# Forgetting attention with split one-pass score products and one shared step for the last queries

## The reference, cut to what matters

```
q = rmsnorm(q, q_gain) * (Dh ** -0.5);  k = rmsnorm(k, k_gain)
c = cumsum(log_sigmoid(f + b_f))              # one row of 272 values per head
s = q @ k.T + c[query] - c[key];  s = where(key <= query, s, -inf)
o = softmax(s) @ v
o = o * sigmoid(gate);  out = o @ w_out
```

## Time and profile before

| | us |
|---|---|
| median of 3 runs | 5328.38 |
| lowest, highest | 5323.99, 5332.9 |
| the profiled execution: time | 5331.09 |
| the profiled execution: span | 5329.3 |
| first attention stage (first POOL instruction to the end of the last gate product) | 3318.25 to 3464.27 |
| second attention stage | 4927.7 to 5073.64 |

### The profile page before, as it was taken

How to read it: one execution, slowest core, us unless ns; L and a number is a source line. 1 busy time by engine, 2 the same in 40 slices (tenths; PEclk the granted TensorE clock), 3 DMA queues, 4 the chain that set the end, 5 groups by cost and what they waited for, 6 DMA issues and landing times. The chain is left out here.

```text
span 5329.3 us, 57668 instructions
## 1 busy us (share of the span) xinstructions
PE 4142.0 (78%) x19870; PEld 2896.1 (54%) x19870; DVE 3009.1 (56%) x6151; ACT 1916.2 (36%) x4273; POOL 1076.5 (20%) x982
## 2 busy tenths in 40 slices
PE   7874677777777777746777768988789967888989
PEld 3663463232232323735323237488789866888489
DVE  7447546676666664475676643354554733544354
ACT  7433323333333333333333334243343421434243
POOL 0015114444444441041444420000100011000000
PEclk9986789999999999868999989599889977999589
DMA  9310139999999996305999963044235400453044
GB/s 365 133 60 0 44 140 420 419 417 416 415 407 417 412 419 241 99 17 188 420 420 415 416 265 109 1 153 152 84 117 164 139 1 1 149 156 116 1 139 139
DMA packets 205764, 1143.63 MB, mean 215 GB/s; under 512 B 24016, under 2 KB 25616, under 8 KB 106784
## 3 DMA queue, kind: packets, MB, share of 16 engines
q0 software_dynamic: 110592, 805.36, 36.7%
q1 hardware_dynamic: 94880, 334.58, 19.0%
HBM read 1138.73 MB, written 1.05 MB: 214 GB/s over the span
## 5 line engine op out<-in xcount | busy, mean ns | idle before, releaser
L1065 PE MATMUL bank<-rows,diag 128*128 128x512 f32 x2304 | 1091.1, 619 | 395.6 <-ACT diag L1120 388.3
L348 PE MATMUL bank<-x_high,w_high 128*128 128x272 f32 (+2 forms) x3560 | 1107.4, 311 | 100.8 <-DVE x_low L414 100.5
L348 PE MATMUL bank<-x_low,w_high 128*128 128x272 f32 (+2 forms) x3560 | 1096.3, 308 | 0.0
L348 PE MATMUL bank<-x_high,w_low 128*128 128x272 f32 (+2 forms) x3560 | 1095.4, 308 | 0.0
L400 DVE TENSOR_TENSOR w_low<-ring,w_high 128x1024 fp32r<-128x1024 f32 (+2 forms) x541 | 645.6, 1200 | 707.9 <-ACT w_high L375 707.9
L1065 PEld LDWEIGHTS bank<-rows,diag 128*128 128x128 f32 x2304 | 426.7, 194 | 1053.0 <-ACT diag L1120 598.8
L1237 DVE CUSTOM_DVE_ANT_0 junk<-rows,hT 128x1024 f32<-128x1024 f32 x576 | 705.7, 1225 | 412.1 <-DMA rows<-in_peer_uv,expert 396.1
L1028 POOL DMA_INDIRECT rows<-in_peer_uv,expert x576 | 622.2, 1080 | 1160.0 <-PE bank L1065 807.3
L348 PEld LDWEIGHTS bank<-x_high,w_high 128*128 128x128 f32 x3560 | 684.0, 192 | 151.0 <-issue 58.2
L375 ACT CAST w_high<-ring 128x1024 fp32r<-128x1024 f32 (+2 forms) x541 | 552.3, 1027 | 583.0 <-PE bank L348 555.1
L348 PEld LDWEIGHTS bank<-x_low,w_high 128*128 128x128 f32 x3560 | 686.3, 193 | 20.5
(11 more groups left out here) (346 smaller groups left out, 4965.7 us busy)
## 6 DMA issues: line engine op xcount, KB each, us to landing
ring<-in_w_gate_up SPq DMA_DIRECT2D x176, 512.0 KB, 3.4
ring<-in_w_mod SPq DMA_DIRECT2D x96, 512.0 KB, 5.7
ring<-in_w_in SPq DMA_DIRECT2D x64, 512.0 KB, 3.4
ring<-in_fox_w_in SPq DMA_DIRECT2D x64, 512.0 KB, 3.4
ring<-in_w_down SPq DMA_DIRECT2D x64, 512.0 KB, 3.5
ring<-in_peer_wq SPq DMA_DIRECT2D x32, 512.0 KB, 3.4
ring<-in_gdn_w_in SPq DMA_DIRECT2D x32, 512.0 KB, 3.8
ring<-in_w_down SPq DMA_DIRECT2D x32, 384.0 KB, 3.8
```

The source lines that it names most:

```text
L348: last = pe.matmul(k.bank[c % BANKS][:, 0:nt], w[:, slot, cols], xx[:, t, t0:t0 + nt], start=(t == 0 and n_pass == 0), stop=(t == KT - 1 a ...
L1065: last = pe.matmul(k.bank[2 * (i % 2) + half][:, :], diag[:, n % 4, :], slot(n)[:, D + half * 512:D + (half + 1) * 512], start=(e == 0), s ...
```

## The change

Three things, in both attention stages. First, q and k are split into float32r halves (`q_high`, `q_low`, `k_high`, `k_low`) by a cast on ACT and a subtraction on DVE per chunk, and a score product becomes three float32r products on 64 rows; the decay is one more float32r product of a broadcast column of ones for the head (`pick`) with `c_rows`, which holds the high parts and the rests of the running sums. The query's own term c[query] is left out. The scores are made negated (the gain of q has a minus sign), so the row's minimum serves directly as the bias of an exponential with scale -1, and the negation step is gone. Second, a step "head" does both blocks of 128 queries of a head in one PSUM bank: 128 keys for the first, 256 for the second. Third, the last 16 queries of four heads share one step "last": their queries are placed in four strips of 32 stationary columns, zero outside the head's rows (`end_high`, `end_low`), and six products of 272 columns on 128 rows over two chunks, with one for the decay, give the scores of the four heads together. So 48 steps become 20. POOL first fills the four zeroed tiles, which all other engines wait for; the DMA and `picked` are gone. The constants grow by 272 columns.

```diff
-    put("causal", np.concatenate([np.zeros((P, 2 * P)), np.where(i[None, :] > i[:, None], NEG, 0.0)], 1))
+    put("causal", np.concatenate([np.zeros((P, 2 * P)), np.where(i[None, :] > i[:, None], -NEG, 0.0)], 1))
+    put("causal_last", np.where(np.arange(T2)[None, :] > 2 * P + (i % 32)[:, None], -NEG, 0.0))
+    put("pick2", sum((i[:, None] == np.arange(FOX_HEADS)[None, :] + r) for r in (0, 32, 64, 96)))
...
-                order(dve.tensor_scalar(k.qgain[:, 0:1], gq, DK_FOX ** -0.5, None, ALU.mult))
+                order(dve.tensor_scalar(k.qgain[:, 0:1], gq, -(DK_FOX ** -0.5), None, ALU.mult))
...
-                order(dve.tensor_scalar(f[:, 2, :], f[:, 1, :], -1.0, None, ALU.mult))
...
-    steps = [(h, i) for h in range(FOX_HEADS) for i in range(3)]
+    steps = []
+    for g in range(4):
+        steps += [("last", g)] + [("head", 4 * g + j) for j in range(4)]
...
+        q_high, q_low = (sbuf(k, es, n, [P, KD, 2 * P], F32R) for n in ("q_high", "q_low"))
+        end_high, end_low = (sbuf(k, es, n, [P, KD, P], F32R) for n in ("end_high", "end_low"))
+        k_high, k_low = (sbuf(k, es, n, [P, KD, T2], F32R) for n in ("k_high", "k_low"))
+        c_rows = sbuf(k, es, "c_rows", [P, T2], F32R)
+        pick = sbuf(k, es, "pick", [P, FOX_HEADS], F32R)
+        pick_last = sbuf(k, es, "pick_last", [P, 4 * P], F32R)
+        sc = sbuf(k, es, "sc", [P, 3, 384])
+        pr = sbuf(k, es, "pr", [P, 3, 384])
+        pT = sbuf(k, es, "pT", [P, 2, 384])
+        pL = sbuf(k, es, "pL", [P, 2, 384])
+        least = sbuf(k, es, "least", [P, 3, 2])
+        total = sbuf(k, es, "total", [P, 3, 2])
+        inv = sbuf(k, es, "inv", [P, 3, 2])
...
+        def end_of(j):
+            return slice((j % 2) * DK_FOX, (j % 2 + 1) * DK_FOX), slice(j // 2, KD, 2), slice(32 * j, 32 * j + META)
         @block.gpsimd
         def _(pool):
+            for ap in (end_high, end_low):
+                pool.tensor_copy(ap[:, :, :], k.causal[:, 0:P].unsqueeze(1).broadcast_to([P, KD, P])).then_inc(s.cleared, 1)
+            pool.tensor_copy(c_rows[:, :], k.causal[:, 0:1].broadcast_to([P, T2])).then_inc(s.cleared, 1)
+            pool.tensor_copy(pick_last[:, :], k.causal[:, 0:1].broadcast_to([P, 4 * P])).then_inc(s.cleared, 1)
...
+            kind, h = steps[n]
+            bank = k.bank[n % 3]
             if n >= 3:
+                pe.wait_ge(s.lowest, n - 2)
+            if kind == "last":
+                pe.wait_ge(s.low, 4 * (h + 1))
+                if n == 0:
+                    pe.wait_ge(s.ends_low, 4)
+                for c in (2 * h, 2 * h + 1):
+                    for i, (qq, kx) in enumerate(((end_high, k_high), (end_high, k_low), (end_low, k_high))):
+                        pe.matmul(bank[:, 0:T2], qq[:, c, :], kx[:, c, :], start=(c == 2 * h and i == 0), stop=False)
+                if n == 0:
+                    pe.wait_ge(s.rows, 4)
+                pe.matmul(bank[:, 0:T2], pick_last[:, h * P:(h + 1) * P], c_rows[:, :], start=False, stop=True).then_inc(s.scored, 1)
+                return
+            own = slice((h % 2) * DK_FOX, (h % 2 + 1) * DK_FOX)
+            for t0, nk in ((0, P), (P, 2 * P)):
+                out = bank[:, t0:t0 + nk]
+                for i, (qq, kx) in enumerate(((q_high, k_high), (q_high, k_low), (q_low, k_high))):
+                    pe.matmul(out, qq[own, h // 2, t0:t0 + P], kx[own, h // 2, 0:nk], start=(i == 0), stop=False)
+                last = pe.matmul(out, pick[own, h:h + 1].broadcast_to([DK_FOX, P]), c_rows[own, 0:nk], start=False, stop=True)
+            last.then_inc(s.scored, 1)
...
+            cuts = (0, 128, 256) if kind == "head" else (0, 128, 256)
+            for j, k0 in enumerate(cuts):
+                nk = P if kind == "head" else TILES2[j][1]
+                last = pe.transpose(bank[0:nk, j * P:(j + 1) * P], pr[:, n % 3, k0:k0 + nk], k.ident)
             last.then_inc(s.turned, 1)
...
+            vv = lambda j: v[0:TILES2[j][1], j, h * DK_FOX:(h + 1) * DK_FOX]
+            t = pT[:, h % 2, :]
+            pe.matmul(bank[lo:lo + DK_FOX, 0:2 * P], vv(0), t[:, 0:2 * P], start=True, stop=False)
+            pe.matmul(bank[lo:lo + DK_FOX, P:2 * P], vv(1), t[:, 2 * P:3 * P], start=False, stop=True)
+            for j in range(3):
+                nk = TILES2[j][1]
+                at = j * P + 32 * (h % 4)
+                last = pe.matmul(bank[lo:lo + DK_FOX, 2 * P:T2], vv(j), pL[0:nk, (h // 4) % 2, at:at + META], start=(j == 0), stop=(j == 2))
             last.then_inc(s.mixed, 1)
...
+            def make_low(c):
+                for x, high, low in ((q, q_high, q_low), (kk, k_high, k_low)):
+                    dve.wait_ge(s.high, 2 * c + (1 if x is q else 2))
+                    n = low.shape[2]
+                    dve.tensor_tensor(low[:, c, :], x[:, c, 0:n], high[:, c, :].bitcast(F32), ALU.subtract).then_inc(s.low, 1)
+            dve.wait_ge(s.cleared, 4)
+            for j in range(4):
+                dve.wait_ge(s.ends_high, j + 1)
+                own, chunks, cols = end_of(j)
+                dve.tensor_tensor(end_low[own, chunks, cols], q[own, chunks, 2 * P:T2], end_high[own, chunks, cols].bitcast(F32),
+                                  ALU.subtract).then_inc(s.ends_low, 1)
+            make_low(0)
+            make_low(1)
+            dve.wait_ge(s.rows, 2)
+            for row in (32, 96):
+                dve.tensor_tensor(c_rows[row:row + FOX_HEADS, :], f[:, 1, :], c_rows[0:FOX_HEADS, :].bitcast(F32),
+                                  ALU.subtract).then_inc(s.rows, 1)
...
+                    for i, (cols, mask) in enumerate(parts(n)):
+                        if mask is None:
+                            allowed = k.const("causal_last")
+                        else:
+                            allowed = k.causal[:, mask:mask + cols.stop - cols.start]
+                        last = dve.tensor_tensor_reduce(sc[:, b, cols], k.bank[b][:, cols], allowed, 1.0, -NEG, ALU.add, ALU.min,
+                                                        least[:, b, i:i + 1])
+                    last.then_inc(s.lowest, 1)
+                if n < NS and n % 5 in (2, 3) and n // 5 < 3:
+                    make_low(2 * (n // 5) + n % 5)
...
+            def make_high(c):
+                act.copy(q_high[:, c, :], q[:, c, 0:2 * P]).then_inc(s.high, 1)
+                act.copy(k_high[:, c, :], kk[:, c, :]).then_inc(s.high, 1)
+            act.wait_ge(s.cleared, 4)
+            for j in range(4):
+                own, chunks, cols = end_of(j)
+                act.copy(end_high[own, chunks, cols], q[own, chunks, 2 * P:T2]).then_inc(s.ends_high, 1)
+            make_high(0)
+            make_high(1)
+            act.copy(pick_last[0:48, :].rearrange("p (h n) -> p h n", n=32), k.const("pick2")[0:48, :].unsqueeze(2).broadcast_to([48, FOX_HEADS, 32]))
+            act.copy(pick[:, :], k.const("pick2"))
+            for row in (0, 64):
+                act.copy(c_rows[row:row + FOX_HEADS, :], f[:, 1, :]).then_inc(s.rows, 1)
...
+                    for i, (cols, _) in enumerate(parts(n)):
+                        last = act.activation(pr[:, b, cols], sc[:, b, cols], ACT.Exp, scale=-1.0, bias=least[:, b, i:i + 1],
+                                              accum_out=total[:, b, i:i + 1])
+                    last.then_inc(s.exped, 1)
+                if n < NS and n % 5 in (1, 2) and n // 5 < 3:
+                    make_high(2 * (n // 5) + 1 + n % 5)
...
+                    if kind == "head":
+                        if h >= 2:
+                            act.wait_ge(s.mixed, h - 1)
+                        last = act.copy(pT[:, h % 2, :], bank[:, 0:384])
+                    else:
+                        if h >= 2:
+                            act.wait_ge(s.mixed, 4 * (h - 1))
+                        act.copy(pL[:, h % 2, 0:256], bank[:, 0:256])
+                        last = act.copy(pL[0:META, h % 2, 256:384], bank[0:META, 256:384])
```

More of the change, by code:

```diff
@@ L1376, in fox_attention @@
     H = k.H
-    steps = [(h, i) for h in range(FOX_HEADS) for i in range(3)]
+    steps = []
+    for g in range(4):
+        steps += [("last", g)] + [("head", 4 * g + j) for j in range(4)]
     NS = len(steps)
[L1379 to L1397, removed]
+    heads_to = [sum(kind == "head" for kind, _ in steps[:n + 1]) for n in range(NS)]
@@ new lines, in fox_attention, with parts @@
+    lasts_to = [sum(kind == "last" for kind, _ in steps[:n + 1]) for n in range(NS)]
+    with ExitStack() as es, stage(k, "attention", "cleared ends_high ends_low high low rows scored lowest exped rcp normed turned copied mixed gated") as (block, s):
+        q_high, q_low = (sbuf(k, es, n, [P, KD, 2 * P], F32R) for n in ("q_high", "q_low"))
[11 more added lines that the diff above has]
+        inv = sbuf(k, es, "inv", [P, 3, 2])
+        def parts(n):
+            if steps[n][0] == "head":
+                return [(slice(0, 128), 256), (slice(128, 384), 128)]
+            return [(slice(0, T2), None)]
+        def end_of(j):
```

(43 more changed lines are left out.)

60 lines of the change are left out of this document (8 added, 52 removed).

## The result

The kernel after takes 5172.74 us in the median of 4 runs (5161.70, 5165.12, 5180.35 and 5181.45), the kernel before 5328.49 (5323.99 to 5332.90) beside it: a ratio of 0.9707 with a 95% interval of 0.9682 to 0.9731.

The account below looks back on a forecast made before the run. PE's own product list at 1.2 GHz was taken to bound the attention stages: 5331.1 - 94.8 + 0.4 = 5236.7, less 2 x 15.6 and 2 x 1 for the clock: 5203.5, less 2.7: 5201, stated as 5204; 8-in-10 range 5160 to 5256.

Parts of the forecast that it names:

- The 128-column pass: Attention scores: a float32r pass of 128 columns costs 0.213 us at 1.2 GHz, set by its weight load.
- rival of a dear pass: Attention scores: 128-column passes cost 0.43 us each, 27.7 us in all; 5261 at the old clock; chance 0.14.
- that of four cycles a column: Attention scores: float32r passes on 64 rows cost like float32 products, making the kernel slower, +54 us, 5383; chance 0.03.
- A head and the shared step: PE's list in an attention stage at 1.2 GHz: 5.07 us a head, 2.72 a shared step, 92.0 in all.
- Begin of the stage: Attention setup: POOL fills, then casts and rests; PE's first product comes 5.8 us into the stage.
- The clock: Attention stages: granted clock rises from 0.50 at a shared step and mostly holds, 15.6 us less a stage; chance 0.45.
- rival of an unchanged clock: Attention stages: the clock stays at 0.50, 5234 us by the median; chance 0.27.
- That of a clock full nearly from the start: Attention stages: full clock nearly from the start, 59 us a stage, 5158 us in all; chance 0.10.
- I take 83 as the mean of both stages: Attention stages: mean length 83 us with a clock rise part of the way, 15.6 below 98.6.
- the three places foreseen: Clock rise at a shared step about 24, 47 or 70 us into an attention stage; stage near 67, 79 or 91.
- The constants' 272 columns, 0.14 MB, are 0.4 us more of loading: Loading of the constants: the wider tile adds 0.4 us, if nothing else hides it.
- term of the projections: Projections behind the attention stages: starting at clock 1.00 saves 1 us on average each, 2 x 1 in all.

Follow-up runs that it names:

- after_again: The changed kernel run once more, unaltered, beside two plain-heads orders on one chip: 5164.47 us over 5 runs, ratio 0.9702.
- plain_heads: Changed kernel with each head's three float32r score passes replaced by one plain float32 product, the split kept for the shared step: 5156.37 us, ratio 0.9673.
- before with the warm-up: Kernel before, with eight float32 products on 128 rows at the head of PE's attention-stage list: 5275.39 us over 4 runs, ratio 0.9888.

## Why the prediction was right, and where it was off

**What bounds it.** PE's own list bounds the stages before and after. Right. At 1.00 PE waits for DVE a little (1.0 us from 3335 to 3375).

**The 128-column pass.** 0.213 forecast, 0.21 measured, with a load on 64 rows as long as on 128. By the rule of the Trainium skill ("TensorE: Matmul & The Clock Gate", section "LDWEIGHTS (loading the stationary operand)") it would have been 0.107; at 0.50 the runs differ from it for these float32r loads. The rival of a dear pass falls, and that of four cycles a column too: 256 columns in 0.21 are one cycle a column.

**A head and the shared step.** 4.98 for 5.07 and 2.52 for 2.72: PE's list at 0.50 is 16 x 4.98 + 4 x 2.52 = 89.8 for 92.0. At 1.00 a head is 2.78 (3347.32 to 3350.10 from product to product) for 2.7. The kernel without the shared step tests the sum at 0.50: its heads are 4.97 apart (4904.22 to 4909.19), 16 of them and its begin of 8.5 make 88.0, where its stages take 87.0 and 87.2. So such sums are good to 1 or 2 us. Begin of the stage 6.0 for 5.8.

**The clock.** The mechanism held: 0.50 in the heads, a rise behind a shared step, kept in one stage of the profile and lost after 10 us in the other. That it is the shared step is shown by the kernel without one (0.50 in both its stages but for 1.0 us) and by the 12 rises counted there. What in it counts, the rows or the dense stream, isn't told apart. The rival of an unchanged clock falls. That of a clock full nearly from the start falls for this kernel, but its price of 59 us a stage is borne out by a relative: the one stage that ran at 1.00 from its setup on took 57.9, with plain heads, earlier casts and the warm-up. The Trainium skill (same page, section "Why this matters for your kernels") ties the full clock to an engine kept busy without pause; after, 52.00 of 52 us busy at 0.50 disagree with it, as the earlier trace rows did.

**The step that was mis-sized** is "I take 83 as the mean of both stages". The profiled execution has 77.6, the one of after_again 67.3. The rise came at the earliest of the three places foreseen, 23.2 to 24.4 us into the stage, in both stages of both profiles; I had weighed all three alike. What remains luck is the fall behind it. In us, forecast against profiled execution: 10.7 of 22.0 lie in the attention stages (136.7 saved, not 126.0). By the parts above some 4 of them are the list's (96.6 a stage at 0.50, where 98.6 stood) and some 7 the clock's (38 for 31.2), each to within 2 us or so.

The forecast's sums have slips beside that. A group of four heads and a shared step that takes 12 us for 23 saves 11, so from 98.6 the three places of the rise give 66, 77 and 88 us, not 67, 79 and 91; the profile's first stage took 66.1. The setup's parts add up to 5.7. The 5158 of the full clock is by the profiled execution; by the median it would be 5155, less another 2 with the projections. Half of the dear case is 5248, not 5256. The break-even of the slower rival is at 3.0 cycles a column, not 3.2. None of them changes which rival falls.

**The step that was wrong** is "The constants' 272 columns, 0.14 MB, are 0.4 us more of loading": 8.8 of the 22.0. The expert stages got 8.4 shorter, and the constants alone do 7 of it. No row of the profile before bore on it, since it compares one layout only. The last 2.5 us lie in the other stages. The term of the projections, 2 us saved, didn't come either: the last product of the projection starts 30.1 and 29.2 us behind the attention stage before, 30.4 and 30.6 after. In the first the clock fell at 3378.3, before the projection's products began, in the second it was at 0.50 up to 4931.3. So 6.2 us were saved elsewhere, which wasn't followed.

**From execution to median** the forecast took 2.7 off and put 3.2 on for the setup, which left 5204 for 5203.5; after's median lies 8.7 below its profiled execution. In that one the second stage lost the clock for 56 us; that the shorter executions kept it longer is likely from after_again (5163.61 us, 7 us lost), but they have no profile. 22.0 + 8.7 + 0.5 are the 31 us.

**What made the gain.** At an unchanged clock a stage would be 96.6 us by my estimate (6.0 + 89.8 + 0.8), 99 of the 149.6 for both. The clock gave some 38 more (2 x 96.6 - 66.1 - 89.1), the expert stages 8. Within the list, the split isn't what pays: a head's scores went from about 5.6 to 2.0 us with it and without, by the decay's product, which was a float32 one per block and is one pass now, by one emptying for three, and by the last 16 queries, which leave every head for a shared step of 0.63 each. These were told apart by argument from the rows and by plain_heads, not each by a run of its own.

**Open.** Why the clock falls in one execution and not in the next at the same work, and which tile's place the gather minds, if it is one's place. Also whether the load or the columns at two cycles each set the 0.21 of a 128-column pass.

## What to carry to other kernels

A stage bound by TensorE at half clock has a second lever beside fewer products: a short dense run of products on all rows among the others can bring the full clock (leave that run out once, to see whether it did). Before splitting float32 products with few columns into three one-pass products, count loads as well as columns: heads of 128 and 256 keys took 2.01 us of scores either way. Compare stages that the change doesn't touch before crediting the whole gain to it.

## What the runs showed of the hardware that I had not expected

A wider tile of constants, by 64 bytes a partition, shortens gather stages of 1294 and 645 us by 5 and 2.

The granted clock of one and the same stream isn't fixed: before with the warm-up held 1.00 for 14 us in one stage and 38 in the other; the second stage of after was at 0.50 for 56 us in one execution and for 7 in another. Runs of after therefore lie 20 us apart (5161.7 to 5181.5), those of before within 9 in the same set (within 13 where 13 runs were taken). A single profile says which level a stretch had, not which level the kernel has there.

With the one-pass heads on 64 rows a level reached by a warm-up was lost within 7 us; with plain float32 heads on 64 rows it was kept through one stage and lost within 7 us in the next; with heads on 128 rows most of both stages was at 1.00.
